# An S5 layer's last state step on one Trainium2 core: the first quarter of the carry spread in two eighths, and a new order of the TensorE work around it

## The reference

```python
lam_bar = jnp.exp(lam * step)
b_bar = ((lam_bar - 1.0) / lam)[..., None] * b
bu = jnp.einsum('blgn,gpn->blgp', uf.astype(jnp.complex64), b_bar)
a = jnp.broadcast_to(lam_bar, (1, seq, S5_GROUPS, S5_STATE))
_, states = lax.associative_scan(_linear_recurrence_combine, (a, bu), axis=1)
y = jnp.einsum('gnp,blgp->blgn', c, states).real + d.astype(f32) * uf
y = jax.nn.gelu(y.reshape(bsz, seq, D_MODEL))
y = y * jax.nn.sigmoid(y @ glu_w.astype(f32) + glu_b.astype(f32))
```

## Time and profile before

| what | value |
|---|---|
| median of 3 runs | 1298.2 us (1297.83 to 1298.96) |
| the profiled execution's own time | 1298.56 us |
| its span in the profile | 1296.8 us |
| granted TensorE clock, mean | 0.999 |
| PE busy | 1251.5 us (97%) |
| DVE busy | 694.8 us (54%) |
| ACT busy | 458.7 us (35%) |
| POOL busy | 69.6 us (5%) |

### The profile page before, as it was taken

How to read it: one execution, slowest core, us unless ns; L and a number is a source line. 1 busy time by engine, 2 the same in 40 slices (tenths; PEclk the granted TensorE clock), 3 DMA queues, 4 the chain that set the end, 5 groups by cost and what they waited for, 6 DMA issues and landing times.

```text
span 1296.8 us, 16028 instructions
## 1 busy us (share of the span) xinstructions
PE 1251.5 (97%) x6237; PEld 1036.6 (80%) x6237; DVE 694.8 (54%) x806; ACT 458.7 (35%) x474; POOL 69.6 (5%) x83
## 2 busy tenths in 40 slices
PE   3979999999999999999999999999999999999997
PEld 3768788888887888888888888888788888887886
DVE  8997864545454444646555465544454444444433
ACT  6724542323233333334233332332234242423232
POOL 6950000000000000000000000000000000000000
PEclk9999999999999999999999999999999999999999
DMA  5273233232322333322323132323333333323331
GB/s 114 84 123 122 83 106 103 86 109 80 114 66 78 91 110 126 115 88 65 106 65 105 65 105 65 98 65 97 98 97 97 97 97 97 97 67 89 89 104 72
DMA packets 148782, 121.01 MB, mean 93 GB/s; under 512 B 5784, under 2 KB 141136, under 8 KB 148752
## 3 DMA queue, kind: packets, MB, share of 16 engines
q1 hardware_dynamic: 144144, 116.92, 29.4%
q10 hardware_dynamic: 4608, 3.67, 1.4%
HBM read 114.29 MB, written 2.10 MB: 90 GB/s over the span
## 4 chain that ended last, share of the span: by engine, by line
PE 87%; POOL 5%; DVE 4%; ACT 1%; issue 1%; DMA 1%; SPq 1%; ACTq 0%; DVEq 0%; POOLq 0%
PE bank L680 25%; PE bank L682 25%; PE bank L681 25%; POOL s_pool_tmp L1605 2%; PE bank L776 2%; PE bank L778 2%; PE bank L777 2%; PE bank L787 1%; DVE w_lo L1134 1%; POOL s_tc L1702 1%; PE bank L804 1%; PE bank L802 1%; PE bank L803 1%; POOL s_tc L1697 1%; DVE tmp L1124 1%
## 5 line engine op out<-in xcount | busy, mean ns | idle before, releaser
L680 PE MATMUL bank<-u_hi,w_hi 128*128 128x512 f32 x960 | 375.2, 391 | 2.0 <-DVE xT L1379 1.1
L682 PE MATMUL bank<-u_hi,w_lo 128*128 128x512 f32 x960 | 373.7, 389 | 0.0
L681 PE MATMUL bank<-u_lo,w_hi 128*128 128x512 f32 x960 | 373.6, 389 | 0.0
L1134 DVE TENSOR_TENSOR w_lo<-w_raw,w_hi 128x2048 fp32r<-128x2048 f32 x112 | 256.7, 2292 | 202.7 <-ACT w_hi L857 202.4
L857 ACT ACTIVATE w_hi<-w_raw 128x2048 fp32r<-128x2048 f32 x112 | 213.5, 1906 | 185.9 <-PE bank L682 145.9
L680 PEld LDWEIGHTS bank<-u_hi,w_hi 128*128 128x128 f32 x960 | 180.3, 188 | 40.3 <-issue 2.0
L682 PEld LDWEIGHTS bank<-u_hi,w_lo 128*128 128x128 f32 x960 | 180.2, 188 | 37.8
L681 PEld LDWEIGHTS bank<-u_lo,w_hi 128*128 128x128 f32 x960 | 180.3, 188 | 37.5 <-issue 0.5
L680 PE MATMUL bank<-h_hi,w_hi 128*128 128x512 f32 x352 | 137.2, 390 | 2.8 <-DVE w_lo L1134 2.8
L681 PE MATMUL bank<-h_lo,w_hi 128*128 128x512 f32 x352 | 136.9, 389 | 0.0
L682 PE MATMUL bank<-h_hi,w_lo 128*128 128x512 f32 x352 | 136.9, 389 | 0.0
(11 more groups left out here) (202 smaller groups left out, 1350.2 us busy)
## 6 DMA issues: line engine op xcount, KB each, us to landing
w_raw<-in_ret_w_qkvg_dram SPq DMA_DIRECT2D x24, 1024.0 KB, 5.0
w_raw<-in_ffn_w_gate_dram SPq DMA_DIRECT2D x22, 1024.0 KB, 5.1
w_raw<-in_ffn_w_up_dram SPq DMA_DIRECT2D x22, 1024.0 KB, 5.1
w_raw<-in_ffn_w_down_dram SPq DMA_DIRECT2D x32, 704.0 KB, 4.3
w_raw<-in_ret_w_o_dram SPq DMA_DIRECT2D x8, 1024.0 KB, 5.2
w_raw<-in_s_glu_w_dram SPq DMA_DIRECT2D x4, 1024.0 KB, 6.3
s<-w_raw SPq DMA_DIRECT2D x40, 64.0 KB, 3.3
s<-in_x_dram ACTq DMA_DIRECT2D x8, 256.0 KB, 8.4
```

Source lines behind the costliest of these rows:

```text
L680: pe.matmul(o, w_hi[w][:, w_cols], hi, start=first, stop=False)
L681: pe.matmul(o, w_hi[w][:, w_cols], lo, start=False, stop=False)
L682: return pe.matmul(o, w_lo[w][:, w_cols], hi, start=False, stop=end)
L1134: dve.tensor_tensor(w_lo[s][:, :], w_raw[:, s, :], w_hi[s][:, :].bitcast(F32), ALU.subtract).then_inc(w_lo_ready[s], 1)
```

## The change

The spread's first quarter (8 pairs, blocks 0 and 1) becomes two parts of 4 pairs; the list `SPREAD_FROM` holds the blocks at which a part starts, and `scan_done` counts to 5 where it counted to 4. On PE, the state products of block 0 move in front of `strips(7)`, and the input products of blocks 6 and 7 move behind the state products of block 5. The computation is the same.

```diff
+SPREAD_FROM = [0, 1, 2, 4, 6]
...
             def y_states(k):
-                if k % 2 == 0:
-                    pe.wait_ge(scan_done, k // 2 + 1)
+                if k in SPREAD_FROM:
+                    pe.wait_ge(scan_done, SPREAD_FROM.index(k) + 1)
...
             y_inputs(2)
             y_inputs(3)
+            pe.wait_ge(seg_done, 2)
+            y_states(0)
             strips(7)
-            pe.wait_ge(seg_done, 2)
             pe.wait_ge(toep_loaded[2], 16 * 2 * STEPS)
             y_inputs(4)
             y_inputs(5)
-            for k in range(4):
-                y_states(k)
+            y_states(1)
+            y_states(2)
+            y_states(3)
+            y_transposed(0)
+            y_transposed(1)
+            y_states(4)
+            y_states(5)
             pe.wait_ge(toep_loaded[3], 16 * 2 * STEPS)
             y_inputs(6)
             y_inputs(7)
-            y_transposed(0)
-            y_transposed(1)
-            for k in range(4, 8):
-                y_states(k)
-                if k % 2:
-                    y_transposed(k - 3)
-                    y_transposed(k - 2)
+            y_transposed(2)
+            y_transposed(3)
+            y_states(6)
+            y_states(7)
+            y_transposed(4)
+            y_transposed(5)
             y_transposed(6)
             y_transposed(7)
...
-            JH, M = J // 4, SEG - 1
-            for part in range(4):
-                js = slice(JH * part, JH * part + JH)
+            M = SEG - 1
+            for part, (k0, k1) in enumerate(zip(SPREAD_FROM, SPREAD_FROM[1:] + [NBLK])):
+                js, JH = slice(JB * k0, JB * k1), JB * (k1 - k0)
```

## The result

The changed kernel takes 1305.11 us (median of 5 runs, 1303.12 to 1306.03) against 1298.96 for the kernel before beside it (5 runs, 1297.83 to 1300.15). The ratio is 1.0045, 95% interval 1.0034 to 1.0057: slower by 0.45%, 6.15 us. I had forecast slower by 2.85 with a range that ends at 1302.6. The direction was right, the size was not.

A forecast was written before the change was run, and what follows sets the result against it. The chain from POOL's end through strips(7), ACT, SP's load and DVE was taken to bound the gated product's start. Late strips +2.85, the rest 0, gave a median of 1301.05; own range 1300.4 to 1301.7, whole 1298.9 to 1302.6.

The forecast's parts named there:

- DVE and POOL take turns by instruction: First eighth in POOL's last round: each DVE product ends behind a POOL instruction; POOL ends at 84.03, the eighth at 85.6.
- The spread longer by 1.0 and hidden: DVE's later quarters end near 101.0 instead of 100.0, covered by DVE's wait for the weights' high part: 0.
- The late inputs worth nothing: Moving y_inputs(6) and (7) behind y_states(5) removes PE's wait of 1.05, but PE is not late: 0.
- `strips(7)` 2.85 later: On PE, strips(7) waits behind y_states(0) and starts at 87.53; the chain to the product gives nothing back: +2.85.
- the third rival: Delay partly given back by emptier DMA engines or because PE's late order bound the start: +1 to +2, chance 0.08.
- The step that failed: On PE, y_states(0) takes 1.88 and the strips 2.29, so strips(7) starts 2.85 late and everything behind moves equally.
- all of that: Behind the product's start at 112.58, PE's nearly pauseless work and its weight loads move as a block.

The follow-up runs named there:

- both filled: Changed kernel and kernel before, each with useless identity transpositions in nearly all of PE's pauses: 1300.58 and 1298.62 us.
- the filled kernel before: Kernel before with useless identity transpositions in PE's pauses (16 before strips(6), 28 before strips(7), 11 before the product): 1298.62 us.
- eighths alone: Kernel before with only the spread's first quarter in two parts, PE's order unchanged: 1298.16 us.
- filler at the strips alone: Changed kernel with useless identity transpositions only in front of strips(6) (16) and y_states(0) (34): 1300.65 us.
- the one filled at the product: Changed kernel with useless identity transpositions only in front of y_transposed(6) (9) and the product (8): 1302.64 us.
- best version, not filled: Kernel before with first quarter in two parts, late inputs of blocks 6 and 7, gate-weight load ahead of part 3, pauses empty: 1296.90 us.
- eighths, filled: Kernel before with the spread's first quarter in two parts and useless transpositions in PE's pauses (16, 23, 6): 1297.94 us.

## Why the prediction was wrong

**DVE and POOL take turns by instruction: right.** POOL ended at 84.06 (84.03 forecast), the four products at 84.28 (84.25), the first eighth at 85.62 (85.6). In the changed kernel's timeline, one product a window, the second one is still held until POOL's product has ended:

```profile
80.50 1.26 DVE L1130 TENSOR_TENSOR s<-s_states,s_seg_powers 128x196 f32<-128x196 f32 x1
...
80.43 1.10 POOL L1611 TENSOR_TENSOR s_pool_tmp<-s_ct,s_c_powers 128x512 f32<-128x512 f32 x1
```

**The spread longer by 1.0 and hidden: right.** It ended at 101.01, and DVE then waited 6.76 for the weights.

**The late inputs worth nothing: right,** by the run with that part alone.

**`strips(7)` 2.85 later: right as a mechanism, too dear in the sum.** At full clock it is 3.1 (87.79 against 84.65, both filled). What it is worth at the end is 1.96. I had written that the transfers and copies behind it give nothing back, and gave the third rival, in which PE's late order is what bound the start and +1 to +2 remain, 0.08. In the profile of the filled kernel before, PE's order does bind, and 0.8 is given back. This error runs against the other: with 1.96 in its place the forecast would have been further off. One reading was wrong as well and cost nothing: 0.41 of 0.56 is three quarters of a product, and not half.

**The step that failed** is the one that priced `y_states(0)` at 1.88 and the strips at 2.29 and let "all of that" move as a block. It took durations from rows at full clock and put them behind other pauses, and the sum had no term for the clock. At full clock the change lengthens PE's wait of 3.71 by 1.0. In the profile of the changed kernel the wait is 3.13 instead, since `strips(6)` at half clock kept PE busy 1.6 longer; with eighths alone, and the same half clock at `strips(6)`, it was 1.45. Behind 3.13 the clock fell, behind 1.45 it didn't. The second pause, in front of the last transpositions, wasn't in the forecast as a price at all.

In numbers, by the medians: 1.96 for the late strips (1300.58 - 1298.62), 2.06 more with the half clock in `y_states(0)` and the strips (1302.64 - 1300.58), and 2.47 more with that at the product (1305.11 - 1302.64), in all 6.49; the kernel before itself lies 0.34 over its filled form, and 6.15 are left. These are steps from kernel to kernel, so that they add up by themselves, and the last two are not independent: filler at the strips alone takes away 4.46, nearly all of both. Of the 2.47, ten matmuls at 0.2 more are 2.0. The rest may be the load, which took 7.89 in the profile of the changed kernel and 7.20 in that of the one filled at the product; no run was made for that alone.

The Trainium skill, page "TensorE: Matmul & The Clock Gate", "HAM oscillation — how this bites in real kernels", tells of a kernel whose waits drop TensorE to half its rate at every tile; the windows above show the same here, 0.50 behind PE's waits. I hadn't weighed it, since the one profile of before showed 1.00 behind its waits.

What stays open: why the same order keeps its clock in one execution and not in the next (the earlier trace rows against the run with late inputs), and so how long a pause this kernel can bear. Behind waits of 2.24 and 3.13 the clock fell in the changed kernel; behind waits of 3.71 and 2.92 (best version, not filled) it stayed up.

## What to carry to other kernels

- An instruction that waits in an in-order queue costs what stands behind it. Before work is moved into another engine's pause, its input must be ready before that pause ends; here DVE's part was itself held back by the engine for which PE was waiting.
- In this kernel a pause of TensorE has two prices, the time and the clock of what follows. Durations from one profile hold for the clock of that profile; a filler in the pause (0.12 us a piece) separates the two in one run.
- A load that stands in a queue behind issues with a late wait is late for no reason of its own. Moving it ahead gave back 5.4 of the 6.15 that the change had cost. Leaving `y_states(0)` behind `strips(7)` gives back more: eighths alone take 1298.16, 6.95 less than the changed kernel.

## What the runs showed of the hardware

Sixteen transpositions of a 128x128 fp32 tile took 1.97, 0.123 each, with the granted clock at 1.00, where I had counted 0.27. The kernel's own 16 transpositions in the earlier trace rows take the same 1.97 and could have told me. The fp32 products of this kernel stand in the trace twice for each instruction of the program, the transpositions once.

SP's eight DMAs of part 3 took from 5.15 (eighths, filled) to 6.27 (best, not filled) to issue in the profiled executions. The load, where it stands behind them, took from 5.83 (fill at the strips only) to 8.06 (eighths, filled) from issue to landing. At an issue of 5.17 (before, filled) the chain behind `strips(7)` runs over PE, at 5.98 over the load.
